# Rebuilding the opening of a one-core kernel: B and C loaded in long rows, E begun early on GpSimd, V products in pairs, norm and mix operands in PSUM

## The reference, cut to what is computed

```python
# x: (256, 1024). First network, one layer:
h = rmsnorm(x, norm_mix)
# S5 mixer: 64 groups of 16 channels, 64 complex states a group
ab = exp(lam * dt); bb = (ab - 1) / lam * B          # per group: (64,), (64, 16)
s_t = ab * s_{t-1} + bb @ h_t[group]                 # a scan over 256 tokens
y = gelu(Re(C @ s) + d_skip * h)
a, g = split(y @ w_glu); x = x + a * sigmoid(g)
x = x + sqrelu_mlp(rmsnorm(x), w1, w2)               # hidden 4096
x = x + (p @ ple_w) * sigmoid(rmsnorm(x) @ ple_gate_w)
x = rmsnorm(x)
# Second network, two layers, with 256 context rows beside the 256 of x:
mod = silu(c) @ w_ada + b_ada                        # 6144 values each for x and ctx
px = modulate(rms_norm(x)) @ w_in                    # the same for ctx
x = x + g_m * mixer(px, ctx)    # Fourier, convolution, grouped-query and
                                # differential attention branches, mixed, @ w_out
x = x + g_f * swiglu(modulate(rms_norm(x)))          # hidden 2816
# ctx likewise in layer 0; the result is rms_norm(x)
```

## Time and profile before

| | |
|---|---|
| median of three runs | 1982.89 us (1982.76 to 1986.4) |
| the profiled execution | 1981.52 us, its span 1979.7 us, mean granted clock 0.981 |
| PE busy | 1906.8 us (96%), 13077 products |
| PEld busy | 1639.1 us |
| DVE busy | 932.6 us |
| ACT busy | 756.2 us |
| POOL busy | 1108.2 us |

### The profile page before, as it was taken

The page is one execution under the profiler, slowest core; times in us unless marked ns, Lnnn a source line. Parts: engine busy times, 40 slices in busy tenths (PEclk is TensorE's granted clock), DMA queues, the critical chain, the costliest instruction groups (busy, mean ns, idle before and its releaser), DMA issues.

```text
span 1979.7 us, 31484 instructions
## 1 busy us (share of the span) xinstructions
PE 1906.8 (96%) x13077; PEld 1639.1 (83%) x13077; DVE 932.6 (47%) x1688; ACT 756.2 (38%) x1212; POOL 1108.2 (56%) x611
## 2 busy tenths in 40 slices
PE   8989999989999999999999999999999998989997
PEld 5578999877887788778878888888788987989997
DVE  7956542254935793752443111114476756382112
ACT  4343553333234523642323222222345536434443
POOL 6426898563535443334543444444368754868885
PEclk8989999989999999999999999999999999999999
DMA  6857766764222132114334323223535331665653
GB/s 167 239 200 238 262 216 213 263 202 161 64 74 86 33 123 69 33 65 138 107 109 147 92 84 119 89 75 105 190 125 156 119 106 43 213 227 174 195 168 99
DMA packets 289490, 276.60 MB, mean 140 GB/s; under 512 B 19802, under 2 KB 276324, under 8 KB 289092
## 3 DMA queue, kind: packets, MB, share of 16 engines
q1 hardware_dynamic: 286804, 271.42, 43.1%
q10 hardware_dynamic: 2192, 2.77, 0.5%
q0 software_dynamic: 352, 0.40, 0.1%
HBM read 266.70 MB, written 4.19 MB: 137 GB/s over the span
## 4 chain that ended last, share of the span: by engine, by line
PE 88%; DVE 5%; ACT 2%; DMA 2%; issue 1%; SPq 1%; POOL 1%; ACTq 0%; DVEq 0%; POOLq 0%
PE gb L2597 19%; PE gb L2599 19%; PE gb L2598 19%; PE gb L1755 3%; PE gb L1756 3%; PE gb L1754 3%; PE gb L1482 3%; PE gb L1484 3%; PE gb L1483 3%; PE mb L1208 1%; DMA raw<-in_w_ada 1%; PE gb L667 1%; PE mb L667 1%; PE mb L1275 1%; PE mb L1355 1%
## 5 line engine op out<-in xcount | busy, mean ns | idle before, releaser
L2584 POOL TENSOR_TENSOR wl<-raw,wh 128x1024 fp32r<-128x1024 f32 (+3 forms) x448 | 978.2, 2202 | 780.1 <-ACT wh L819 779.8
L819 ACT CAST wh<-raw 128x1024 fp32r<-128x1024 f32 (+3 forms) x452 | 420.2, 938 | 651.8 <-PE gb L2599 375.6
L2597 PE MATMUL gb<-xh,wh 128*128 128x256 f32 (+1 forms) x1856 | 602.5, 325 | 10.6 <-DVE xl L1158 5.3
L2598 PE MATMUL gb<-xl,wh 128*128 128x256 f32 (+1 forms) x1856 | 598.5, 322 | 0.0
L2599 PE MATMUL gb<-xh,wl 128*128 128x256 f32 (+1 forms) x1856 | 598.4, 322 | 0.0
L2597 PEld LDWEIGHTS gb<-xh,wh 128*128 128x128 f32 x1856 | 350.7, 189 | 46.9 <-issue 11.7
L2599 PEld LDWEIGHTS gb<-xh,wl 128*128 128x128 f32 x1856 | 350.7, 189 | 27.5
L2598 PEld LDWEIGHTS gb<-xl,wh 128*128 128x128 f32 x1856 | 350.9, 189 | 27.2
L1754 PE MATMUL gb<-fhh,wh 128*128 128x512 f32 (+1 forms) x352 | 118.4, 336 | 0.0
L1756 PE MATMUL gb<-fhh,wl 128*128 128x512 f32 (+1 forms) x352 | 117.9, 335 | 0.0
L1755 PE MATMUL gb<-fhl,wh 128*128 128x512 f32 (+1 forms) x352 | 117.9, 335 | 0.0
(11 more groups left out here) (475 smaller groups left out, 3020.2 us busy)
## 6 DMA issues: line engine op xcount, KB each, us to landing
raw<-in_w_in SPq DMA_DIRECT2D x62, 1024.0 KB, 5.3
raw<-in_w_ada SPq DMA_DIRECT2D x48, 1024.0 KB, 5.5
raw<-in_w_ffn SPq DMA_DIRECT2D x44, 1024.0 KB, 5.2
raw<-in_mlp_w SPq DMA_DIRECT2D x32, 1024.0 KB, 5.6
raw<-in_w_ffn SPq DMA_DIRECT2D x16, 768.0 KB, 4.3
raw<-in_w_ffn SPq DMA_DIRECT2D x16, 640.0 KB, 4.1
raw<-in_ssm_w_glu SPq DMA_DIRECT2D x8, 1024.0 KB, 7.1
raw<-in_w_out SPq DMA_DIRECT2D x8, 1024.0 KB, 4.8
```

The source lines that it names most:

```text
L819: nc.scalar.copy(split_half(wh, p, j, h), raw_half(p, it, j, h)).then_inc(hi_ready, 1)
L2584: nc.gpsimd.tensor_tensor(split_half(wl, p, j, h), raw_half(p, it, j, h), split_half(wh, p, j, h).bitcast(F32), ALU.subtract)\
L2597: nc.tensor.matmul(o, H[:, k, :], XH, start=st, stop=False)
L2598: nc.tensor.matmul(o, H[:, k, :], XL, start=False, stop=False)
```

## The change

- *Loads.* B is read in two transfers with whole rows (`Bq`, issued by ScalarE) and turned by 32 transposes of 32 rows; C in two transfers with whole rows into `cnat`, turned by 32 products with columns of the identity that separate the groups' parity; the gain as one row (`rowg`), spread by two products with ones. x (`xnat`) is issued second in SP's queue. C's turn comes first on TensorE behind B's; x is transposed in two halves, after u.
- *Order.* The rms root and its mask stand ahead of `Bb` on VectorE. GpSimd starts with E as soon as `Ct` is there, gives `s_sk` behind the first E group, computes the chunk powers behind the second, and does seven half groups; VectorE does one and no `e_last`. `sc` (silu of c) moves to VectorE.
- *V loop.* F is transposed and copied for two pairs at a time (four transposes, one copy, eight products). Eight ada blocks stand in it one by one, and the first half of K (`K_FIRST`). The fillers of the opening fall from 21 + 2 + 7 to 2 + 9.
- *Ring.* 12 ada blocks are loaded ahead of the gate tiles; the zeros of toep stand behind the fifth load and wait for `s_U`.
- *Scan.* Its temporaries and factors stand in PSUM, its last ones in `w1` and unused columns of `x`.
- *Gate tiles.* The low parts of both go to GpSimd; the high part of the second is taken by ScalarE inside the y loop. Two ada blocks stand in that loop instead of four.
- *Behind the opening.* The tiles of the norms (except norm 2) and of the fourth branch's mix go to PSUM banks of `mb`, with waits on VectorE for their reuse. In layer 1 the norm ahead of the ffn gives two leading halves instead of three, and the split of the last tile of `wo` moves behind the norm's copies. Fillers: three more in norm 7, three in each pass of the grouped attention, four in the differential one.

```diff
-        EARLY_ADA, EARLY_GLU = 10, 2
+        EARLY_ADA, EARLY_GLU = 12, 2
...
-        BEFORE_ZEROS = 4
+        K_FIRST = 9
+        BEFORE_ZEROS = 5
...
-                sp.wait_ge(s_U, 1)
+                sp.wait_ge(s_xg, CH)
...
-            sp.wait_ge(s_lnat, 16 * 3)
...
-            for ri, name in enumerate(("ssm_b_re", "ssm_b_im")):
-                bn = A[name][0].rearrange("(q g) p h -> (g p) q h", g=2)
-                for r in range(2):
...
+            sp.dma_start(xnat[:, :, :], A["x"][0].rearrange("(a p) d -> p a d", p=P)).then_inc(s_xnat, 16)
+            for ri, name in enumerate(("ssm_c_re", "ssm_c_im")):
+                sp.dma_start(cnat[:, ri, :, :], A[name][0].rearrange("(r g) h p -> (g h) r p", g=8)).then_inc(s_cnat, 16)
             for j in range(CH):
                 sp.dma_start(h32[:, CH - 1 - j, :], xc[j]).then_inc(s_h32[j // 2], 16)
-            sp.dma_start(xnat[:, :, :], A["x"][0].rearrange("(a p) d -> p a d", p=P)).then_inc(s_xnat, 16)
...
             sp.wait_ge(s_vz, 4)
-            sp.wait_ge(s_ss, 1)
-            sp.wait_ge(s_ct5, 1)
+            sp.wait_ge(s_U, 1)
...
-                unused_products(2 if n == 7 else 1)
+                unused_products(4 if n == 7 else 1)
...
+                return lambda k, part: ring[:, k % 4, part]
+            banks = {0: (1, 3), 1: (1, 2)}.get(n, (1, 2, 3))
+            return lambda k, part: mb[:, banks[k % len(banks)], part]
...
                 if k < KD:
+                    free = 2 if n in (0, 1) else 3
+                    if n != 2 and k >= free:
+                        dve.wait_ge(s_xl, op0[n] + k - free + 1)
...
                     _, _, t, h, keys, c0 = ITEMS[mine[i][0]]
+                    if i == 1:
+                        if c0 >= 4:
+                            pe.wait_ge(s_ex, c0 - 3)
+                        unused_products(3, gb[:, c0 % 4, 0:2 * P])
...
                 if i == 2:
                     pe.wait_ge(s_qtl, TN[l, "d"] + 8)
                     pe.wait_ge(s_qv, l + 1)
+                    unused_products(4, mb[:, mine[0] % 2, 0:2 * P])
...
-                            lead=() if half else THREE)
+                            lead=() if half else THREE[0:3 - l])
...
-            gemm_act(act, q["wo"], lambda it, j: None, tail=lambda: squares_act(act, n0 + 2, sqr2))
...
+        def mixed_pair(l, pair):
+
+            return mb[:, 2 * (pair % 2):2 * (pair % 2) + 2, 0:layer_T(l)]
...
+                        if b == 3 and pair > 1:
+                            dve.wait_ge(s_ml, 8 * l + 2 * (pair - 1))
...
                         dst = mix[:, 2 * pair:2 * pair + 2, 0:T]
-                        prod = dst if b == 0 else two(pr2, s_, T)
+                        prod = dst if b == 0 else mixed_pair(l, pair) if b == 3 else two(pr2, s_, T)
...
+            for ri, name in enumerate(("ssm_b_re", "ssm_b_im")):
+                act.dma_start(Bq[:, ri, :, :, :], A[name][0].rearrange("(q g) p h -> q g p h", g=2)).then_inc(s_Bq, 16)
...
+            for j in range(4):
+                x_by_group(j)
+            act.wait_ge(s_ct5, 1)
+            act.wait_ge(s_vz, 2)
+            nc.scalar.copy(Ct[:, 0, :, 0:GH], gb[:, 1, :].rearrange("p (q h) -> p q h", h=GH)).then_inc(s_Ctc, 1)
+            nc.scalar.mul(Ct[:, 1, :, 0:GH], gb[:, 2, :].rearrange("p (q h) -> p q h", h=GH), -1.0).then_inc(s_Ctc, 1)
+            for j in range(4, CH):
+                x_by_group(j)
+            act.wait_ge(s_fp5, 1)
+            nc.scalar.copy(fac[:, :], gb[:, 2, 0:NCH]).then_inc(s_fac, 1)
+            for i in range(2):
+                act.wait_ge(s_xt, i + 1)
+                nc.scalar.copy(x[:, 4 * i:4 * i + 4, 0:SEQ],
...
-                nc.scalar.copy(w1[:, q % 4, :, :], gb[:, 1 + q % 2, 0:256].rearrange("p (r m) -> p r m", r=2))\
-                    .then_inc(s_w1, 1)
-                if q % 8 == 0 and q:
-                    v_copy(q // 8 - 1)
...
+            for b in range(PAIRS // 2):
+                act.wait_ge(s_w1t, b + 1)
+                if b >= 2:
+                    act.wait_ge(s_w1u, b - 1)
+                nc.scalar.copy(w1[:, 2 * (b % 2):2 * (b % 2) + 2, :, :],
+                               gb[:, 1 + b % 2, :].rearrange("p (a r m) -> p a r m", a=2, r=2)).then_inc(s_w1, 1)
+                if b % 4 == 0 and b:
...
+            pool.wait_ge(s_pw, 1)
             pool.wait_ge(s_Ctc, 2)
...
-            pool.wait_ge(s_U, 1)
             e_half(0, 0)
-            pool.wait_ge(s_th, 1)
...
+            pool.wait_ge(s_Bt, 1)
+            nc.gpsimd.memset(zeros[:, :, :], 0.0).then_inc(s_vz, 1)
             e_half(0, 1)
             pool.sem_inc(s_E, 1)
+            pool.wait_ge(s_Db, 48)
+            pstep(g_.tensor_tensor(Db, Db, Dg, ALU.mult))
+            g_.tensor_tensor(Db, Db, const[0:GH, C_EYE:C_SEL].unsqueeze(1).unsqueeze(1)
+                             .to_broadcast([GH, 4, GH, GH]), ALU.mult).then_inc(s_sk, 1)
+
             e_half(1, 0)
             e_half(1, 1)
             pool.sem_inc(s_E, 1)
+            chunk_powers()
             e_half(2, 0)
+            e_half(2, 1)
+            pool.sem_inc(s_E, 1)
+            e_half(3, 0)
             pool.sem_inc(s_E, 1)
             pool.wait_ge(s_S, 1)
@@ -2569,10 +2599,6 @@
...
+            warm(2, 2)
+            pe.wait_ge(s_Bq, 16 * 2)
+            for ri in range(2):
+                for h in range(GH):
+                    ins = nc.tensor.transpose(gb[:, 3 * ri, PAIRS * h:PAIRS * h + PAIRS],
+                                              Bq[:, ri, :, :, h].rearrange("q g p -> q (g p)"), ident[0:PAIRS, 0:PAIRS])
+            ins.then_inc(s_Bt, 1)
+            pe.wait_ge(s_cnat, 16 * 2)
+            of_parity = ident.rearrange("p (q g h) -> p g q h", q=4, g=2)
+            for ri in range(2):
+                for r in range(8):
+                    for g in range(2):
+                        ins = nc.tensor.matmul(gb[64 * g:64 * g + 64, 1 + ri, 64 * r:64 * r + 64],
...
+            pe.wait_ge(s_Bb, 1)
             pe.wait_ge(s_small, 32)
             pe.wait_ge(s_chk, 1)
...
+            pe.wait_ge(s_xnat, 16)
+            pe.wait_ge(s_fac, 1)
+            for i in range(2):
+                if i:
+                    pe.wait_ge(s_x1, 1)
+                for k in range(4):
+                    for a in range(2):
+                        ins = nc.tensor.transpose(gb[:, 1 + k // 2, (k % 2) * 256 + a * P:(k % 2) * 256 + a * P + P],
+                                                  xnat[:, a, (4 * i + k) * P:(4 * i + k) * P + P], ident)
...
+                    pe.wait_ge(s_F, b // 4 + 1)
+                    pe.wait_ge(s_F0, 2 * (b // 4 + 1))
+                if b >= 2:
+                    pe.wait_ge(s_w1, b - 1)
+                for e in range(2):
+                    q = 2 * b + e
+                    for ri in range(2):
+                        ins = nc.tensor.transpose(gb[:, 1 + b % 2, (2 * e + ri) * P:(2 * e + ri + 1) * P],
+                                                  Fg[q // 8][:, q % 8, ri, :, :], ident)
                 ins.then_inc(s_w1t, 1)
...
+                pe.wait_ge(s_w1, b + 1)
+                for q in (2 * b, 2 * b + 1):
+                    for ri in range(2):
+                        for g in range(2):
+                            c = (q % 8) * 64 + ri * 32
+                            ins = nc.tensor.matmul(mb[64 * g:64 * g + 64, q // 8, c:c + NCH],
+                                                   w1[:, q % 4, ri, 64 * g:64 * g + 64], U[:, 2 * q + g, :],
+                                                   start=True, stop=True)
...
-                banks = (gb[:, 1:3, :], mb[:, 2:4, :])[i]
...
+            for b in range(PAIRS // 2 + 1):
+                if b < PAIRS // 2:
+                    w1_transposes(b)
+                if b:
+                    v_products(b - 1)
+                if b in (4, 6, 8, 10, 12, 14):
+                    if b == 4:
+                        pe.wait_ge(s_sc, 1)
+                    for n in {4: (0, 1), 6: (2,), 8: (3,), 10: (4,), 12: (5, 6), 14: (7,)}[b]:
+                        ada_block(pe, n)
+                if b == K_FIRST:
+                    pe.wait_ge(s_Vc, 2)
+                    k_products(0)
+            pe.wait_ge(s_w1, PAIRS // 2)
             k_products(1)
-            ada_block(pe, 5)
-            pe.wait_ge(s_sk, 1)
-            for b in range(2):
-                nc.tensor.matmul(mb[:, b, :], ident[0:GH, :],
-                                 Db.rearrange("p k (q b) h -> p b k q h", b=2)[:, b], start=True, stop=False)
-            ada_block(pe, 6)
+            skip_products()
             k_back(0)
             k_back(1)
-            for n in range(7, EARLY_ADA):
+            for n in range(8, 12):
                 ada_block(pe, n)
-            warm(7, 1)
+            warm(9, 1)
...
+                late = ((), (), (), (0,), (), (1,), (), ())[d]
...
+            dve.sem_inc(s_pw, 1)
+            dve.wait_ge(s_ss, 1)
+            dve.wait_ge(s_Ctc, 2)
```

(30 more changed lines are left out.)

317 lines of the change are left out of this document (126 added, 191 removed).

## The result

The changed kernel takes 1989.57 us (median of 20 runs, 1980.78 to 1995.14), the kernel before 1982.83 in as many beside it; the ratio is 1.0035, 95% interval 1.0022 to 1.0048. The forecast was 1960.

What follows compares the result with a forecast made beforehand. Bound: a chain across all engines up to 126.11 us, TensorE behind it. From the profiled 1981.5 us, -15.6 until glu and -7.6 behind the opening gave 1958.3; 1.4 under the median, so 1960. Own range 1952 to 1966, chance 0.62.

Steps and rivals of the forecast that it cites:

- SP's queue: Zeros of toep behind block 4's load: seven issues end by 54, land by 60, hidden by 8 us.
- no other new entry on a queue: Chain of waits up to y: besides the zeros on SP, the change adds no entry that delays it.
- Gate tiles' low parts to GpSimd: Low parts of both gate tiles move to GpSimd along with VectorE's last E work; forecast as hidden.
- The copies: Seven copies inside toep, issued at 82, landed at 91, some 2 us ahead of y at 92.8.
- The rival of the late copies: Copies take 13.8 us from K's copies: y at 96, total 1963; behind loads 101.6, 1968; chance 0.09.
- The clock: V loop bound 77 if TensorE's first quarter ran low; rival: lower level throughout 46 to 92, total 2003, chance 0.03.
- Ct and U: Opening: Ct copied at 16.3 us against 40.6 before; U starts at 35.1, behind GpSimd's work.
- the scan's 19.6 us: Scan on VectorE keeps its 19.6 us with temporaries in PSUM, from 73.1 to 92.7.
- the bound of F3 plus a quarter: V loop cannot end before F group 3 (62.5) plus its last quarter (9.0): 71.5 us; 72.0 taken.
- The y loop: Seven steps of 2.34 and 1.3: 17.7 us instead of 24.5, without the 3.09 wait; glu at 110.5.
- Behind the opening: Behind the first glu product, norm and mix tiles in PSUM plus fillers: -7.6 us, bounds -2 and -14.

Runs made afterwards that it cites:

- moved: Changed kernel with zeros behind the fourth load, gate low parts on VectorE, ada blocks 4-7 behind K, 8-13 in y loop, copies before block 8's load; 1980.25 us.
- calm: Changed kernel with toep's zeros behind the fourth load and all twelve modulation blocks behind the K products; 1996.83 us, one execution, only its trace used.
- behind2: Repetition of behind, unedited; 1977.51 us, ratio 0.9979 to the kernel before.
- k15: Changed kernel with the first half of the K products behind the 15th instead of the 9th pair of pairs; 1987.63 us, one execution.
- nofill: Changed kernel with zeros behind the fourth load, first two gate tiles' low parts on VectorE, two instead of nine fillers ahead of y; 1979.90 us, ratio 0.9984.
- fed4: Changed kernel with zeros behind the fourth load, six fillers ahead of the V loop, blocks 0 and 1 before the F group 1 wait; 1985.14 us, ratio 1.0006.
- ring10: Changed kernel with 10 modulation blocks, then both gate tiles, loaded ahead of the copies inside toep, and four blocks in the y loop; 1990.65 us, ratio 1.0043.
- behind: Kernel before with only the part of the change that lies behind the opening; 1979.68 us, ratio 0.9976.
- opening: Changed kernel with the part behind the opening undone, so only the new opening; 1996.28 us, ratio 1.0060.

## Why the prediction was wrong

The first glu product of the profiled execution came 23.3 us later than forecast. Of these 13.6 arose up to the end of the V loop, 2.8 between there and y, and 6.9 in the y loop. Behind it the timed runs gain some 3 us less than forecast.

1. *SP's queue: the step that failed most.* "Seven issues end by 54 and land by 60 ... Hidden by 8 us." They were issued from 54.0 to 62.7 and landed until 69.6. Of the 8.7 us by which the last issue was late, 6 come from the start: block 0, whose use frees the slot, was used at 53.5 and not at 48, since F group 1 came 3.3 us late and TensorE was at the lower level. The other 2.7 are the issues' own time, 8.69 where 6 had been allowed; the kernel before had shown 7.64 (the line below). The zeros themselves held nobody up, since the scan came only at 86.7; the loads of blocks 5 and up stood behind them and kept the engines full. Put back: 6.7 us.

```profile
42.06 7.64 SPq L753 DMA_DIRECT2D toep<-zeros  x7
```

2. *Code, which no term had.* The prediction found "no other new entry on a queue"; this one is on no queue of the program: TensorE's own instructions come over the DMA engines, in packets of 16 KB. With the engines full and the late zeros the wait was 3.45 to 4.90 us in five executions, with the early zeros 1.32 to 3.34 in seven (and none in moved), with no load in flight (calm) none. Full engines alone do not make it: the kernel before had them at 1.02 to 1.09 of their share from 50 to 65 us and no such wait (behind2, with the same opening, one of 0.79), and moved had full ones from 55 to 61 and no such wait. What else it takes is not shown; K's first half, new in the V loop, was suspected, and k15 settles it only in part. The Trainium skill (Runtime: NRT & Kernel Launch, Instruction fetch mechanics) has the same 16 KiB blocks, each sequencer fetching them by its own DMA queue, and calls their cost mostly hidden. The 4.90 us say that it need not be.

3. *Gate tiles' low parts to GpSimd, forecast at nothing.* The argument that two SBUF sources make VectorE stand still beside GpSimd stood further down, for the norms, and was not held against the y loop, where the change itself puts GpSimd beside such instructions. Put back: 3.7 us, at the edge of what the runs can tell. The Trainium skill (SBUF — State Buffer, Who interferes with whom) says that a VectorE instruction with two SBUF inputs contends with a GpSimd instruction that reads SBUF; the 2737 ns beside 413 agree.

4. *The copies: 9 us forecast from K's copies to the last landing, 11.7 measured, 12 to 13 to y.* "Seven issues of 0.6 and 5 for 1.8 MB" takes the weights' rate for the transfer; the copies ran at 0.12 to 0.28 MB a us. The rival of the late copies was close ("if they need 13.8 us"), and no load has to be in flight for it. The fillers ahead of y are covered by it: without them (nofill) y waits as long.

5. *The clock* was at the lower level for nearly all that TensorE did from 11 to 55 us, which only a bound and a rival had, and again from 73 to 78, behind the wait of 4.90 us. Raising it ahead of the V loop bought nothing that the timed runs show (fed4). It was not free in every stretch: with F group 3 long done, the four steps of two pairs' transposes or products from 73.5 to 77.6 took 4.1 us, and the like from 80.2 to 82.6 took 2.4; calm gives some 2 us too. Both are estimates from one execution. *Ct and U* were 2.9 and 3.2 us late, the scan's 19.6 us came out at 19.6 with its operands in PSUM, and the bound of F3 plus a quarter is met when little else stands in the loop (moved: 72.9, with a wait of 0.16 us for F group 3).

6. *The y loop: 17.7 forecast, 24.6 measured,* 20.3 to 22.2 with the low parts repaired. One part of the rest was in no term: with 12 blocks ahead of them, the gate tiles' loads stand behind the copies, so ScalarE waited for the first tile until 113.1 and split it (2.43 us) ahead of the first gelu, while VectorE stood for 4.56 us; in the kernel before this tile had landed at 89.0. ring10 undid the order and lost as much elsewhere. moved shows why an earlier y is not an earlier glu: 14 blocks and two gate tiles of 1 MB must be loaded, used and split ahead of the glu gemm through four slots. Started 7 us sooner than before, the loop took 29.0. Where the blocks stand changed the place of the waiting, and no arrangement tried came out ahead of the old opening: ratios of 0.9981 to 1.0043 with the part behind, which alone gives 0.9976 and 0.9979.

7. *Behind the opening: -7.6 forecast,* 4.0 and 4.4 measured by the medians (behind, behind2), and 4 to 5 by the ratios of opening and the changed kernel. That VectorE no longer stands still holds: the view by source line that answers the earlier trace rows has 425 ns as its maximum, the four subtractions of the earlier trace rows take 1.42 us instead of 7.75, and TensorE's waits for `xl` behind the first glu product fall from 8.8 to 4.0. All its waits there fall from 44.1 to 35.9, but most of the rest of this is filled and not gained: 80 fillers instead of 48 stand there, and take 23.5 us instead of 14.9. The profiled executions do not show the gain: behind and behind2 take 1853.0 and 1853.6 us behind the first glu product, before 1853.6. The 4 us rest on the timed runs, and which of the edits gives them, and which term of the 7.6 was too large, was not separated.

Open stays why the timed executions of the changed kernel are 6 to 9 us above its two profiled ones. The clock is a candidate, since behind the opening the same instructions took 1845 us in one execution and 1853 in another; it is not shown, since no long execution of the changed kernel was profiled. Open stays also what share of the 6.7 us is the load's and what the code's: in both cases it is the same transfers, and they were not separated. The version to keep is behind, 4 us faster than before. The view of item 7, to be held against the earlier trace rows:

```profile
L1159 DVE TENSOR_TENSOR xl<-mb,xh x16: 417/417/425, 190.2 to 402.5; 128x256 fp32r<-128x256 f32 x16
```

## What to carry to other kernels

A transfer moved on a queue takes the duration of its new neighbourhood, and all that stands behind it is late by that; charge it against the first use behind it, not against its own. When work moves to another engine, list what the new engine will run beside, and apply to it every contention that was found elsewhere in the same kernel. Before a start is priced by its dependencies, add up what must flow through the ring until the next big gemm; if that binds, an earlier start only moves the wait.

## What the hardware showed that was not expected

- TensorE's waits of 1 to 5 us without a semaphore, while the DMA engines are full: in twelve executions TensorE goes on 1.2 to 1.5 us after a packet of 16 KB of instructions has ended. None with idle engines in calm, and none in the V loops of before and moved, though their engines were near full.
- Copies inside SBUF of 1.8 MB in seven transfers: 12 to 13 us until their reader starts, in ten executions, the last landing 0.2 to 0.7 us ahead of it. In nofill they move 0.12 to 0.28 MB a us in packets of 4 KB, with no weights beside them, where weights in packets of 1 KB reach 0.36.
- Doubling TensorE's clock for 10 us of the V loop did not shorten the kernel.
- The granted clock can fall for some us while TensorE is busy throughout, in one execution and not in another with the same instructions (0.62 and 0.70 against 1.00 near 790 us); behind the opening such executions took up to 7.7 us longer.
